# Every remainder of the weight split on VectorE, in unit order, and none on GpSimd

## The reference

```
h = h + 0.5 * rmsnorm(swiglu(rmsnorm(h, g[0]), ffn1_w_in[i], ffn1_w_out[i]), g[1])
u = rmsnorm(h, g[2])
mix = even_mixer(u, ...) if i % 2 == 0 else odd_mixer(u, ...)
h = h + rmsnorm(mix, g[3])
h = h + 0.5 * rmsnorm(swiglu(rmsnorm(h, g[4]), ffn2_w_in[i], ffn2_w_out[i]), g[5])
gate = jax.nn.sigmoid(h @ ple_w_gate[i])
h = h + rmsnorm(gate * (p[i] @ ple_w_proj[i]), g[6])
```

## Time and profile before

| what | before |
|---|---|
| median of three runs | 1611.33 us |
| span of the profiled execution | 1609.2 us |
| TensorE busy | 1477.0 us, 92% |
| VectorE busy | 852.5 us, 53% |
| ScalarE busy | 706.2 us, 44% |
| GpSimd busy | 377.8 us, 23% |
| mean granted clock of TensorE | 0.955 |

### The profile page before, as it was taken

How to read it: one execution, slowest core, us unless ns; L and a number is a source line. 1 busy time by engine, 2 the same in 40 slices (tenths; PEclk the granted TensorE clock), 3 DMA queues, 4 the chain that set the end, 5 groups by cost and what they waited for, 6 DMA issues and landing times.

```text
span 1609.2 us, 17128 instructions
## 1 busy us (share of the span) xinstructions
PE 1477.0 (92%) x6606; PEld 1212.3 (75%) x6606; DVE 852.5 (53%) x757; ACT 706.2 (44%) x692; POOL 377.8 (23%) x153
## 2 busy tenths in 40 slices
PE   3999889898999988889999989999999979999896
PEld 3788677676888877667887867878888848888785
DVE  8734775866334457446434474452673343654344
ACT  2545747334344436134444344443443443444332
POOL 3122212213122222003112131222322332322112
PEclk9999999999999999579999999999999979999998
DMA  6745234645455453106544455554643522654441
GB/s 270 292 157 210 105 105 156 236 157 201 162 200 185 163 224 142 46 1 216 184 163 167 179 204 188 209 192 147 234 177 141 206 105 105 229 184 163 169 163 40
DMA packets 40508, 272.51 MB, mean 169 GB/s; under 512 B 4865, under 2 KB 5889, under 8 KB 8834
## 3 DMA queue, kind: packets, MB, share of 16 engines
q1 hardware_dynamic: 36992, 261.65, 44.5%
q10 hardware_dynamic: 3458, 10.04, 1.8%
HBM read 270.62 MB, written 1.05 MB: 169 GB/s over the span
## 4 chain that ended last, share of the span: by engine, by line
PE 73%; DVE 15%; ACT 5%; POOL 3%; issue 3%; DMA 2%; DVEq 0%; SPq 0%; ACTq 0%; POOLq 0%
PE acc L1741 22%; PE acc L1743 22%; PE acc L1742 22%; DVE wlo L1047 5%; PE turn L1794 3%; ACT whi L367 2%; POOL wlo L920 2%; DMA raw<-in_units 1%; DVE h L1117 1%; DVE xn L1101 1%; DVE gate_part L1435 1%; DVE feed_lo L1085 1%; DVE red L1178 0%; DMA gpost<-in_norm_g 0%; PE turn L1895 0%
## 5 line engine op out<-in xcount | busy, mean ns | idle before, releaser
L1047 DVE TENSOR_TENSOR wlo<-raw,whi 128x2048 fp32r<-128x2048 f32 x175 | 463.6, 2664 | 346.5 <-ACT whi L367 346.5
L1741 PE MATMUL acc<-whi,feed_hi 128*128 128x512 f32 (+1 forms) x1504 | 605.8, 403 | 38.9 <-DVE wlo L1047 15.9
L1743 PE MATMUL acc<-whi,feed_lo 128*128 128x512 f32 (+1 forms) x1504 | 593.3, 394 | 0.0
L1742 PE MATMUL acc<-wlo,feed_hi 128*128 128x512 f32 (+1 forms) x1504 | 593.2, 394 | 0.0
L367 ACT ACTIVATE whi<-raw 128x2048 fp32r<-128x2048 f32 x233 | 445.3, 1916 | 326.6 <-PE acc L1743 298.2
L1741 PEld LDWEIGHTS acc<-whi,feed_hi 128*128 128x128 f32 x1504 | 288.6, 192 | 103.2 <-DVE wlo L1047 16.2
L1743 PEld LDWEIGHTS acc<-whi,feed_lo 128*128 128x128 f32 x1504 | 288.0, 191 | 61.9
L1742 PEld LDWEIGHTS acc<-wlo,feed_hi 128*128 128x128 f32 x1504 | 288.9, 192 | 57.3 <-issue 0.2
L928 POOL TENSOR_TENSOR wlo<-raw,whi 128x2048 fp32r<-128x2048 f32 x29 | 133.9, 4618 | 519.9 <-ACT whi L367 519.9
L920 POOL TENSOR_TENSOR wlo<-raw,whi 128x2048 fp32r<-128x2048 f32 x29 | 141.1, 4867 | 393.1 <-ACT whi L367 393.1
L1741 PE MATMUL acc<-whi,hid_hi 128*128 128x512 f32 x352 | 137.8, 392 | 0.0
(11 more groups left out here) (302 smaller groups left out, 1011.4 us busy)
## 6 DMA issues: line engine op xcount, KB each, us to landing
raw<-in_units SPq DMA_DIRECT2D x245, 1024.0 KB, 4.9
gpost<-in_norm_g ACTq DMA_DIRECT2D x8, 512.0 KB, 4.4
gpre<-in_norm_g ACTq DMA_DIRECT2D x6, 512.0 KB, 6.4
h<-in_x SPq DMA_DIRECT2D x1, 1024.0 KB, 5.9
w_ax<-in_w_ax SPq DMA_DIRECT2D x1, 1024.0 KB, 9.2
bgate<-in_b_gate SPq DMA_DIRECT2D x1, 1024.0 KB, 11.4
out<-h SPq DMA_DIRECT2D x2, 512.0 KB, 2.6
decay<-in_decay ACTq DMA_DIRECT2D x1, 768.0 KB, 4.1
```

Of the source, the lines that this page charges most:

```text
L1047: dve.tensor_tensor(wlo[:, u % RING, :], raw[:, u % RING, :], whi[:, u % RING, :].bitcast(F32), ALU.subtract).then_inc(lo_ready, 1)
L1741: pe.matmul(out, xh, wh, start=first, stop=False)
L1742: pe.matmul(out, xh, wl, start=False, stop=False)
L1743: return pe.matmul(out, xl, wh, start=False, stop=last)
```

## The change

`by_pool` and `rest_count` go. The counter `pool_lo` goes; all waits on a remainder are on `lo_ready`, at the unit's number plus one. VectorE's `lo` no longer skips a unit, and all of GpSimd's remainders are taken out of its program, which keeps the roots and the elementwise products. The operation and its operands are the same on either engine.

```
-            signal, per_turn = (pool_lo, 1) if by_pool(u) else (lo_ready, RING - 1)
-            engine.wait_ge(signal, rest_count(u) if it is None else it * per_turn + rest_count(u))
+            engine.wait_ge(lo_ready, u + 1 if it is None else it * RING + (u + 1))
...
-            def lo():
-
-                u = n["u"]
-                n["u"] += RING
-                pool.wait_ge(hi_ready, u + 1)
-                pool.tensor_tensor(wlo[:, RING - 1, :], raw[:, RING - 1, :], whi[:, RING - 1, :].bitcast(F32),
-                                   ALU.subtract).then_inc(pool_lo, 1)
...
-                for _ in range(5 if half == 0 else 3):
-                    lo()
...
-                lo_through(stage)
-                norms(stage)
+                norms()
...
                     if u >= U_TOTAL:
                         return
-                    if by_pool(u):
-                        continue
                     dve.wait_ge(hi_ready, u + 1 if it is None else it * RING + (u + 1))
                     dve.tensor_tensor(wlo[:, u % RING, :], raw[:, u % RING, :],
                                       whi[:, u % RING, :].bitcast(F32), ALU.subtract).then_inc(lo_ready, 1)
```

More of the change, by code:

```diff
@@ L70, in raw_of @@
     return u + N_MOD1 + (N_MOD2 if u >= U_GATE else 0)
[L73 to L80, removed]
 G_Q, G_K, G_XZ0, G_V, G_ZA, G_XZ1, G_GR, G_GA, G_OA, G_OR, G_WO = range(11)
@@ L274, in build @@
         lo_ready = sem("lo_ready")
-        pool_lo = sem("pool_lo")
         unit_used = sem("unit_used")
@@ L889, in _ @@
         def _(pool):
-            n = {"step": 0, "ss": 0, "ssm": 0, "pre": 0, "u": RING - 1}
+            n = {"step": 0, "ss": 0, "ssm": 0, "pre": 0}
             def step(ins):
@@ L913, in rstd_pre, with norms @@
                     .then_inc(pre_rstd, 1)
-            def lo():
-                u = n["u"]
-                n["u"] += RING
-                pool.wait_ge(hi_ready, u + 1)
-                pool.tensor_tensor(wlo[:, RING - 1, :], raw[:, RING - 1, :], whi[:, RING - 1, :].bitcast(F32),
-                                   ALU.subtract).then_inc(pool_lo, 1)
[L923 to L934, removed]
+            def norms(pre=True):
                 for t in range(TOK):
                     rstd()
-                    if t == (0 if first else 1):
-                        lo()
                     if pre:
@@ L960, in _ @@
                     .then_inc(mod_pooled, 1)
-            stage = U_IN + U_OUT
             for half in range(2):
-                for _ in range(5 if half == 0 else 3):
-                    lo()
                 pool.wait_ge(decay_done, half + 1)
@@ L972, in _ @@
                                    ALU.mult).then_inc(kept_decay, 1)
-            for _ in range(3):
-                lo()
-            norms(stage)
+            norms()
             for layer in range(2):
-                stage += U_FFN_IN + U_FFN_OUT
-                lo_through(stage)
-                norms(stage)
+                norms()
                 if layer == 0:
-                    stage += U_EVEN_IN + U_EVEN_OUT
                     pool.wait_ge(even_loaded, 16 * 5)
-                    lo()
                     for t in range(TOK):
@@ L988, in _ @@
                                            .to_broadcast([P, A_HEADS, P]), ALU.mult).then_inc(gated, 1)
-                        if t == 0:
-                            lo()
-                    lo()
                     for t in range(TOK):
@@ L994, in _ @@
                 else:
-                    stage += U_ODD_IN + U_ODD_OUT
                     pool.wait_ge(odd_loaded, 16 * 2)
-                    for _ in range(4):
-                        lo()
                     for pair in range(2):
@@ L1004, in _ @@
                                                .to_broadcast([P, 2, C_DV]), ALU.mult).then_inc(gated, 1)
-                            if t == 0:
-                                lo()
                     for i in range(2 * TOK):
                         rstd_heads(i, 2, C_DV)
[L1009 to L1014, removed]
+                norms()
+                norms(pre=False)
                 if layer == 0:
-                    norms(stage)
-            assert n["u"] >= U_TOTAL
+                    norms()
             rstd(2)
```

## The result

The changed kernel takes 1556.1 us (median of four runs, 1550.9 to 1560.2) against 1611.0 us before: a ratio of 0.967, 95% interval 0.964 to 0.970. The profiled execution has a span of 1558.1 us; 1558.5 were predicted for it. Five more runs, beside the last experiment, gave 1560.0 us. Executions of this one kernel differ by 9 us: of the four, two took 1560.0 and 1560.2 us (mean granted clock 0.968 and 0.966), two 1552.2 and 1550.9 (0.974 and 0.975); the profiled one is of the longer kind, and the median lies between.

A forecast was written before the change was run, and what follows sets the result against it. TensorE, busy 1477.0 of 1609.2 us, was taken as the bound. Place-by-place gains summed to 50.7 us (about 32 waiting, 18 clock), giving a span of 1558.5; 2.1 more for the median gave 1561, range 1549 to 1584.

The forecast's parts named there:

- 187: TensorE's 3.70 us wait for `yat` at 187.03: wins 1.9 of waiting plus 1.7 of clock, 3.6 us.
- 862: The 2.42 us wait ahead of 862.23: followed by clock 1.00, so no clock loss; 0 in the sum.
- 1504: TensorE's 3.74 us wait at 1504.17: two remainders and the multiplication end earlier, wins 1.3 plus 2.5 of clock, 3.8 us.
- 952: TensorE's 4.91 us wait at 952.26 for blocked `xn` (L1101): wins 4.2 plus 1.7 of clock, 5.9 us.
- Rival B: Waits shrink, but remaining gaps of 1.3 to 2.4 us at six places still lower the clock: 1579 us; chance 0.17.
- The seams of the odd mixer: Into and out of the odd mixer, `scale_out` and TensorE's next rows come 0.5 us later each: 1.0 us lost.
- F: More comes back than counted, from VectorE's 65 us of blocked time in waits left alone: 1550 us; chance 0.07.
- I cost it at nothing in the loops: Added remainders in feed-forward loops cost nothing, covered by two more TensorE units (about 5.4 us); uncovered, up to 2.3 a group.
- The cover of 0.1 us: Last full feed-forward group: the delayed multiplication `hid` ends at about 494.95, TensorE needs it at 495.03.
- C: GpSimd's small roots are blocked by VectorE remainders at nine seams, up to 21 us: 1582 us; chance 0.06.
- D: VectorE's in-order queue becomes the bound; slower if over 38% of the added 133 us is exposed, 1626 at half; chance 0.05.
- E: VectorE's long instructions have another cause than GpSimd, so the change does not free it: 1611 us; chance 0.03.

The follow-up runs named there:

- the last experiment: On one chip, five rounds: the kernel after with two reorderings, 1542.2 us, beside the kernel after unchanged, 1560.0 us.
- experiments 1 to 4: 1: kernel after plus unread GpSimd differences, 1621.4 us; 2: fills instead, 1559.6; 3: before, fills replacing GpSimd's remainders, 1551.1; 4: the third with longer fills, 1561.6.
- experiments 1 to 6: First four: see experiments 1 to 4; 5: kernel after, 58 moved remainders computed twice, 1607.5 us; 6: GpSimd keeps 29 remainders inside feed-forward stages, 1563.0.
- experiment 3: Kernel before, but GpSimd fills its units' remainder slots with zeros instead of computing them; VectorE keeps its 175: 1551.1 us.
- Experiment 5: Kernel after with each of the 58 moved remainders computed twice on VectorE, the unit given out after the second: 1607.5 us.
- experiment 1: Kernel after, plus a GpSimd difference of two SBUF operands into an unread spare tile at the 58 old places: 1621.4 us.
- the reordered kernel: Kernel after with one weight unit moved behind each second feed-forward's silu and multiplication, and a remainder moved into block 1's root wait: 1548.1 us, later 1542.2.

## Why the prediction was right, point by point

**The mechanism.** Right, and experiments 1 to 4 show it: GpSimd's two-input instructions on SBUF lengthen VectorE's. What was predicted of the profile came: 233 remainders without a long tail, L1060 and L1044 at 0.75 and 0.69 us, no wait over 3 us at 345, 571, 737, 952 and 1580. One reading of the prediction was inexact: "both end when GpSimd ends". By the earlier trace rows GpSimd ends at 571.87 and the addition at 572.42, 0.55 later. At the longest remainder of before it is 2.15 us (GpSimd until 343.46, VectorE until 345.61):

```profile
338.50 4.96 POOL L920 TENSOR_TENSOR wlo<-raw,whi 128x2048 fp32r<-128x2048 f32 x1 [16.99 <-ACT whi L367]
338.94 6.67 DVE L1047 TENSOR_TENSOR wlo<-raw,whi 128x2048 fp32r<-128x2048 f32 x1
```

By these figures the blocked instruction stands still until GpSimd is done, and then takes nearly its own length (0.75 and 2.29).

**The size.** 50.7 predicted, 51.1 measured in the profiled pair. That they agree to 0.4 us is in part luck: the profiled execution is one of the longer ones, and two of the other three were 8 to 9 us shorter, which the prediction did not reckon with. The median, 1556.1, is 5 us under the 1561 that was predicted. Ten of the terms are within 0.4 us. The errors of the others cancel, and most of them are one mistake about the clock:
- 187: 3.6 predicted, 1.9 measured. The clock is 1.00 in 187 to 193 (0.72 before), though it is 0.65 in 181 to 184 now; but VectorE gives `yat` only 1.65 us sooner (with the 0.27 us that the kernel after was behind until there, that is the 1.9), and TensorE waits for it again, 1.48 us at 194.30. Inside this chain, which VectorE sets, TensorE's clock is worth nothing. The step "clock 1.7" was wrong, not "wins 1.9".
- 862, 1504 and 952: the step "2.42 us left the clock at 1.00" was read from one place. In nine profiled executions (before, after twice, and experiments 1 to 6) there are 14 waits of 2.40 to 2.43 us ahead of the embedding's first matmul; the window of 6 us behind them has the clock at 0.72 in six and at 1.00 in eight, in code that the experiments leave alone. Four of the six belong to the kernel after, which had 0.72 at both places in both of its profiles; whether that is chance is open. It cost 1.6 us each and explains -1.6 at 862 and 2.2 instead of 3.8 at 1504. At 952 the gap that is left is the 1.46 us at 911.51, and the clock behind it is 0.72 too, so that only a part of the 1.7 us of clock came back. Rival B was thus partly at work. It was priced at six places and 18 us and came true at three, for some 4.
- The seams of the odd mixer, -1.0 predicted: a wait of 0.4 us is there at four seams, two of them these (one of the others is shown, 553.06), but in the distances between the traces no loss stands out.
- 3.5 us came from places that the sum did not have: short waits behind blocked instructions and pieces of low clock. This is F in small.

**The queue.** "I cost it at nothing in the loops" holds: the 133 us cost 5 to 9 by experiment 3, and the kernel after has no wait of 0.3 us or more inside a feed-forward. Part of that was in the sum already, as the 2.29 us that the places were charged with. The cover of 0.1 us was 0.33. Experiment 5 shows that at this place the margin is all there is: of 2.29 us more, 1.96 were exposed.

**The rivals.** C's mechanism exists (L891 at 1.88 us in place of 0.19) and costs next to nothing: L1053 covers it at the seam shown, and all of VectorE's waits for these roots are 7.0 us in the kernel after against 6.5 before. The prediction priced it from L904, the root inside `scale_out`; the row just ahead of that one, beside the remainder at 564.43, already showed it:

```profile
565.48 1.29 POOL L903 TENSOR_SCALAR ms<-ss 128x1 f32<-128x1 f32 x1 [2.15 <-ACT xn L387]
```

D's threshold of 38% was not reached (4 to 7% exposed), but the next 133 us come to 37%. E fell with experiment 1.

## What to carry to other kernels

Judge work that is given to GpSimd by what it does to VectorE: 58 instructions of 4.6 us lengthened VectorE's by 93 us and the kernel by some 50, while their own lateness cost 10 to 14. An instruction on a fixed shape with a maximum two or three times its median is the sign; the cause is the instruction of the other engine inside which it starts, and after whose end it takes about its usual length. And price moved work by what stands behind it in the queue at its tightest place, since the first 133 us were nearly free and the second cost 50.

## What the runs showed of the hardware that I had not expected

- A GpSimd fill of 1.8 us, or three in a row to 4.6 us, does not slow VectorE (mean 2293 ns); a GpSimd difference of two SBUF operands does, though it reads the same 110 columns over and over (mean 2810 ns). The Trainium skill, SBUF — State Buffer, section Who interferes with whom, has this rule: a VectorE instruction with two SBUF inputs contends with a GpSimd instruction that reads SBUF, not with one that only writes. By these runs it holds.
- The block is whole, not a slowing: VectorE's remainder ends 2.14 to 2.16 us after the end of GpSimd's instruction at each of the 16 places in the trace of before where one that stands by itself in the timeline starts inside it.
- The block is not on all of VectorE's work. `feed_lo`, with one operand in PSUM, has a maximum of 693 ns in experiment 1, and four of its instructions lie wholly inside one of GpSimd's; two of them here:

```profile
1156.18 3.58 POOL L928 TENSOR_TENSOR junk<-ident 128x1760 bf16<-128x1760 f32 x1 [2.75 <-ACT whi L372]
1157.99 1.29 DVE L1086 TENSOR_TENSOR feed_lo<-turn,feed_hi 128x512 fp32r<-128x512 f32 x2 [1.20 <-ACT feed_hi L414]
```

  L1118, on SBUF alone, rises from 748 to 1047 ns in the mean. The same section says that a VectorE instruction with at most one SBUF input, outside its two-port modes, does not contend; the 693 ns agree.
- The granted clock behind a wait of 2.4 us is not settled by the wait: 0.72 in six of 14 cases, 1.00 in eight. The level through the even mixer differs too between executions of one program (0.50 throughout, or 1.00 for part of it), and it makes 7.5 of the 8.0 us between two executions of the reordered kernel.
